# One weight tile in eight multiplied in full fp32, and the softmax row sums kept in SBUF instead of PSUM

## What is computed

```python
z = jnp.einsum('bhqd,bhkd->bhqk', qi, k).astype(jnp.float32) * scale
causal = key_pos[None, :] <= q_pos[:, None]
p = jax.nn.softmax(jnp.where(causal, z, neg), axis=-1)
return jnp.einsum('bhqk,bhkd->bhqd', p.astype(v.dtype), v)
```

## Time and profile before

| | |
|---|---|
| median of three runs | 2393.22 us (2389.26 to 2399.34) |
| profiled execution | 2389.26 us, of which 2387.6 us are the span of its instructions |
| mean granted TensorE clock, whole span | 0.913 |
| busy over the whole span | PE 1971.5 us, DVE 1342.3 us, ACT 952.6 us, POOL 595.2 us |
| MLA stage | 529 us, from 1646 to 2175 us |

### The profile page before, as it was taken

One profiled execution on the slowest core, in us unless ns is written; L12 is line 12 of the kernel. 1 busy time (PEld: TensorE's weight loads), 2 busy tenths in 40 slices (PEclk: granted clock), 3 DMA queues, 4 the chain that ended last, 5 costly groups with the idle time before them and its releaser, 6 DMA issues. The chain is left out here.

```text
span 2387.6 us, 32025 instructions
## 1 busy us (share of the span) xinstructions
PE 1971.5 (83%) x9698; PEld 1593.0 (67%) x9698; DVE 1342.3 (56%) x2006; ACT 952.6 (40%) x1876; POOL 595.2 (25%) x555
## 2 busy tenths in 40 slices
PE   6589999967777547755989888896999999995998
PEld 1368888856666446653766666674878788784786
DVE  2711111121111158876999999996888888884111
ACT  2411111121111123334666666664767676674000
POOL 1400000000000025540000000003767777673221
PEclk9699999978888779987999999996999999997999
DMA  7245543343323136666334251408315243404554
GB/s 276 85 132 175 165 127 127 110 166 106 110 103 107 74 112 197 201 199 151 71 87 103 53 130 32 110 22 181 72 38 120 56 106 79 115 8 152 176 176 158
DMA packets 220289, 284.59 MB, mean 119 GB/s; under 512 B 10736, under 2 KB 158496, under 8 KB 214544
## 3 DMA queue, kind: packets, MB, share of 16 engines
q1 hardware_dynamic: 217872, 274.96, 39.7%
q10 hardware_dynamic: 2304, 8.39, 0.9%
HBM read 164.56 MB, written 114.56 MB: 117 GB/s over the span
## 5 line engine op out<-in xcount | busy, mean ns | idle before, releaser
L1856 POOL TENSOR_TENSOR mla_wl<-mla_w,mla_wh 128x512 fp32r<-128x512 f32 (+1 forms) x320 | 373.8, 1182 | 152.7 <-ACT mla_wh L1892 145.1
L1488 DVE TENSOR_TENSOR_SCAN sb_w<-sb_kp,sb_w 128x512 f32<-128x512 f32 x192 | 245.2, 1277 | 7.2 <-ACT sb_kp L1438 0.9
L1447 ACT ACTIVATE sb_wh<-sb_pt 128x512 fp32r<-128x512 f32 (+1 forms) x320 | 170.5, 533 | 151.4 <-PE sb_pt L1580 147.5
L1891 ACT ACTIVATE mla_w<-mla_zt 128x512 f32<-128x512 f32 (+1 forms) x320 | 170.7, 533 | 119.9 <-PE mla_zt L2045 59.1
L515 PE MATMUL pt_po<-h_hi,pt_wh 128*128 128x512 f32 x512 | 200.5, 392 | 7.8 <-DVE pt_wl L476 7.8
L516 PE MATMUL pt_po<-h_lo,pt_wh 128*128 128x512 f32 x512 | 200.3, 391 | 0.0
L517 PE MATMUL pt_po<-h_hi,pt_wl 128*128 128x512 f32 x512 | 200.1, 391 | 0.0
L1933 DVE TENSOR_REDUCE mla_nmx<-mla_zn 128x1 f32<-128x512 f32 (+2 forms) x320 | 191.7, 601 | 11.2 <-PE mla_zn L2012 7.8
L1438 ACT ACTIVATE sb_kp<-sb_z 128x512 f32<-128x512 f32 (+3 forms) x320 | 169.7, 531 | 51.4 <-PE sb_z L1558 22.2
L716 PE MATMUL pn_pv<-pn_wh,pn_hs 128*128 128x512 f32 x256 | 104.5, 497 | 86.2 <-DMA pn_hs<-hT 86.2
L1580 PE MATMUL sb_pt<-sb_ident,sb_w 128*128 128x128 f32 x1088 | 174.6, 276 | 0.0
(11 more groups left out here) (221 smaller groups left out, 4381.9 us busy)
## 6 DMA issues: line engine op xcount, KB each, us to landing
pn_hs<-hT SPq DMA_DIRECT2D x16, 1024.0 KB, 11.2
mod_wada<-in_w_ada SPq DMA_DIRECT2D x6, 2048.0 KB, 8.4
qk_mla<-lat_th SPq DMA_DIRECT2D x32, 384.0 KB, 4.3
qk_mla<-lat_tl SPq DMA_DIRECT2D x32, 384.0 KB, 5.1
mod_x<-in_x ACTq DMA_DIRECT2D x16, 512.0 KB, 4.0
pt_w<-in_w_feat SPq DMA_DIRECT2D x16, 512.0 KB, 6.0
hT<-h_hi SPq DMA_DIRECT2D x16, 512.0 KB, 3.5
hT<-h_lo SPq DMA_DIRECT2D x16, 512.0 KB, 5.1
```

What stands on the lines that cost most here:

```text
L1447: nc.scalar.activation(wh[x % RING][:, lo:GW], pt[x % PTS][:, lo:GW], ACT.Copy, bias=-1.0).then_inc(s_hi if plan.split[x] else s_whole, 1)
L1488: nc.vector.tensor_tensor_scan(kept, keeps, keeps, 1.0 if u["n"] == 0 else w[u["g"]][:, u["r"], b:b + 1], ALU.mult, ALU.bypass).then_inc(s ...
L1856: nc.gpsimd.tensor_tensor(wl[i][:, cols], w[i][:, cols], wh[i][:, cols].bitcast(F32), ALU.subtract).then_inc(s_lo, 1)
L1891: nc.scalar.activation(w[i][:, cols], zt[x % 2][:, cols], ACT.Exp).then_inc(s_w, 1)
```

## The change

Two things are edited in `attend_mla` and its plan.

First, every eighth turn of a head (x = 7, 15, 23, 31, 39) is no longer split. ACT makes only w for it, POOL does nothing, and PE multiplies w with v as plain fp32, in one matmul instruction in place of two. Three of the five turns are of full width, two (15 and 39) have 128 columns.

Second, the running sum stays in the SBUF tile acc from the first turn on; the PSUM tile pa is gone. Its bank becomes a tile pm of its own for the transposed row maxima, so that some waits around the shared tile ps are dropped.

```diff
+    WHOLE = 8
...
+                split = len(self.turns) % self.WHOLE != self.WHOLE - 1
...
-        pa = m.ps("pa", [P, GW])
+        pm = m.ps("pm", [P, GW])
...
             def low(it, hp, x):
+                if not plan.turns[x]["split"]:
+                    return
...
-                pool.wait_ge(s_wh, turns(x, it, hp) + 1)
+                pool.wait_ge(s_wh, split_turns(x, it, hp))
...
-                nc.scalar.activation(wh[i][:, cols], zt[x % 2][:, cols], ACT.Exp).then_inc(s_wh, 1)
+                if plan.turns[x]["split"]:
+                    nc.scalar.activation(wh[i][:, cols], zt[x % 2][:, cols], ACT.Exp).then_inc(s_wh, 1)
...
-                nc.scalar.activation(qh[hp][QK:KP, g * GW:(g + 1) * GW], ps[0:1, :], ACT.Copy).then_inc(s_row, 1)
+                nc.scalar.activation(qh[hp][QK:KP, g * GW:(g + 1) * GW], pm[0:1, :], ACT.Copy).then_inc(s_row, 1)
...
-                if tn["first"]:
-                    nc.vector.tensor_copy((a if tn["diag"] else pa)[:], w[x % RING][:]).then_inc(s_acc, 1)
-                    return
-                dve.wait_ge(s_acc, turns(x, it, hp))
-                into = a if tn["diag"] else pa
-                came = a if tn["lowest"] else pa
-                nc.vector.tensor_tensor(into[:, cols], came[:, cols], w[x % RING][:, cols], ALU.add).then_inc(s_acc, 1)
+                    nc.vector.tensor_copy(a[:], w[x % RING][:]).then_inc(s_acc, 1)
+                else:
+                    dve.wait_ge(s_acc, turns(x, it, hp))
+                    nc.vector.tensor_tensor(a[:, cols], a[:, cols], w[x % RING][:, cols], ALU.add).then_inc(s_acc, 1)
...
-                reached(pe, s_scale, groups(n, it, hp) - (1 if n == 1 else 2))
...
-                pe.wait_ge(s_lo, turns(x, it, hp) + 1)
+                if not tn["split"]:
+                    pe.wait_ge(s_w, turns(x, it, hp) + 1)
+                    nc.tensor.matmul(out, vj.bitcast(F32), w[x % RING][:, lo:GW], start=tn["first"],
+                                     stop=tn["last"]).then_inc(s_pv, 1)
+                    return
+                pe.wait_ge(s_lo, split_turns(x, it, hp))
...
-                rows = groups(n, it, hp) + (2 if n == G - 1 else 3)
-                reached(pe, s_row, min(rows, 2 * PAIRS * G) if isinstance(rows, int) else rows)
```

More of the change, by code:

```diff
@@ L1640, in __init__ @@
             for j in range((g + 1) * QG):
-                self.turns.append(dict(n=n, g=g, j=j, lowest=max(0, j - g * QG), diag=(j >= g * QG),
+                split = len(self.turns) % self.WHOLE != self.WHOLE - 1
+                self.turns.append(dict(split=split, n=n, g=g, j=j, lowest=max(0, j - g * QG), diag=(j >= g * QG),
                                        first=(j == 0), last=(j == (g + 1) * QG - 1)))
@@ L1648, in __init__, with splits_to @@
         self.T, self.G = len(self.turns), len(self.groups)
+        self.splits = sum(tn["split"] for tn in self.turns)
+    def splits_to(self, x):
+        return sum(tn["split"] for tn in self.turns[:x + 1])
     def at(self, x, kinds, delays):
@@ L1753, in groups, with split_turns @@
             return it * (2 * G) + (hp * G + n)
+        def split_turns(x, it, hp):
+            return it * (2 * plan.splits) + (hp * plan.splits + (plan.splits_to(x) if x >= 0 else plan.splits_to(x + T) - plan.splits))
         def pair_groups(n, it):
@@ L1948, in add_up @@
                 dve.wait_ge(s_w, turns(x, it, hp) + 1)
-                if tn["diag"] and tn["lowest"] == 0:
+                if tn["first"]:
                     reached(dve, s_sum, groups(tn["n"], it, hp) - 1)
-                if tn["first"]:
-                    nc.vector.tensor_copy((a if tn["diag"] else pa)[:], w[x % RING][:]).then_inc(s_acc, 1)
-                    return
-                dve.wait_ge(s_acc, turns(x, it, hp))
-                into = a if tn["diag"] else pa
-                came = a if tn["lowest"] else pa
-                nc.vector.tensor_tensor(into[:, cols], came[:, cols], w[x % RING][:, cols], ALU.add).then_inc(s_acc, 1)
+                    nc.vector.tensor_copy(a[:], w[x % RING][:]).then_inc(s_acc, 1)
+                else:
+                    dve.wait_ge(s_acc, turns(x, it, hp))
+                    nc.vector.tensor_tensor(a[:, cols], a[:, cols], w[x % RING][:, cols], ALU.add).then_inc(s_acc, 1)
             def halves(it, hp, n):
@@ L2021, in to_row @@
                 reached(pe, s_row, groups(n, it, hp))
-                reached(pe, s_scale, groups(n, it, hp) - (1 if n == 1 else 2))
                 for r in range(QG):
-                    tp = nc.tensor.transpose(ps[0:1, r * P:(r + 1) * P], nm[n % 2][:, r:r + 1], ident[:])
+                    tp = nc.tensor.transpose(pm[0:1, r * P:(r + 1) * P], nm[n % 2][:, r:r + 1], ident[:])
                 tp.then_inc(s_pm, 1)
@@ L2036, in scores @@
                     pe.wait_ge(s_row, groups(tn["n"], it, hp) + 1)
-                reached(pe, s_wh, turns(x, it, hp) - 1)
+                if plan.turns[x - 2]["split"]:
+                    reached(pe, s_wh, split_turns(x - 2, it, hp))
+                else:
+                    reached(pe, s_w, turns(x, it, hp) - 1)
                 lo, g, keys = tn["lowest"] * P, tn["g"], slice(tn["j"] * P, (tn["j"] + 1) * P)
```

## The result

The changed kernel takes 2411.3 us (median of five runs, 2410.6 to 2416.3), the kernel before 2393.3 (five runs, 2389.3 to 2399.3). The ratio is 1.0074, with an interval of 1.0052 to 1.0094: **slower by 18 us**, where +37 was forecast. The sign and the range held; the size was twice too large. The profiled execution took 2413.95 us with a span of 2412.0, 24.4 us more than the span before. The whole of it lies in the MLA stage: its first tile is worked on at 1623.2 us before and 1623.0 after, its last is done at 2178.7 before and 2203.1 after.

The account below looks back on a forecast made before the run. PE was taken to set the pace, DVE just behind. Terms 11 + 0 + 0 + 4 + 20 + 5 = 40 us on 2389.26 gave 2429, forecast as 2430 us; range 2400 to 2482 us.

Parts of the forecast that it names:

- Where the loss comes from: Signs expected in the MLA profile: longer additions and POOL subtractions, DVE busier, ACT's quotient wait above 27 us, earlier stages unchanged.
- Whole products: PE in unsplit turns: fp32 product adds 0.39 us per full-width turn, 0.10 per narrow one; +11.0 us, bounds 0 and 20.
- Whole turns on ACT and POOL: ACT loses 14.2 us and POOL 31.6 us of work; PE waits for POOL only 2.3 us: 0, at best 10 off.
- Rival D: Group ends: the SBUF addition goes while POOL's subtraction waits, the quotient follows directly; faster, 2364 us, chance 0.06.
- The sum beside POOL: SBUF additions queue behind POOL at the port: +4 us in plain turns, +20 at odd heads' closing steps, +5 for clock.
- my terms without the clock: Port delays in the MLA stage: 0.5 us for a head, +4 us; 1.25 us for each of 16 group ends, +20.
- The narrow turns then let DVE catch up: Even heads: 0.8 us of delay left after the longest run is recovered in narrow turns, so most is absorbed.
- 1.2 us in hand: Full-width turns: how late DVE may be before PE wants the zn buffer again, about 1.2 us and no more.
- Clock: MLA stage: longer stalls lower the granted clock, a fifth more loss; +5 us, bounds -15 and +15.
- the prediction's own conversion: Stage clock 0.95 read as a tenth of 529 us at half speed, a loss of up to 26 us.

Follow-up runs that it names:

- e10: The kernel before, plus one semaphore increment that nobody reads on POOL ahead of each subtraction: 2369.7 us, ratio 0.9911.
- the narrow subtraction: The changed kernel with POOL's subtraction cut to the last 128 columns of each tile: 2370.9 us, ratio 0.9894.

## Why the prediction was right in sign and wrong in size

- **Where the loss comes from: right.** Additions of 1.076 us (0.95 to 1.1 expected), subtractions of 1.542, DVE +55 us (60), ACT's wait for the quotient 35.4 us (above 27), the stages before unchanged. Whoever is first at the port runs at full speed and the other stands, as the two rows 0.07 us apart, the quotients of `e10` and the narrow subtraction show. The Trainium skill states this lock on its page "SBUF — State Buffer", section "🔬 SBUF: two separate sides"; the traces agree.
- **Whole products, +11 us: right in kind, over in size.** The 0.39 us for each stands: without relief turn 10 of the first head, which holds the whole product of turn 7, takes 1.80 us in place of 1.40. In the whole kernel it is +6.7 us; where the other 4 went was not looked for.
- **"Whole turns on ACT and POOL ... so I take 0": this step failed.** It is the main error. I priced the relief by PE's waits for POOL, 2.3 us, and its best case at 10. The work that ACT and POOL no longer do is worth about 10 us in the change, and a thing that the diff does beside it, a register instruction more ahead of each subtraction, another 14, much of it by way of the clock. The second I never looked at: I listed the changed wait and priced only what it waits for, not when POOL would then start. Rival D had the mechanism, but put it down to the additions and gave it 0.06.
- **The sum beside POOL, 4 + 20 + 5 = 29 us: too small.** Alone it costs 38. As heads are cut in the table, three of the four closings fall into the odd head and one into the even head behind it, so my terms without the clock are 4.3 us for an odd head, 0.5 for the first head and 1.8 for the other even ones. Measured: odd heads +4.9, +9.4 and +6.3, the first head +2.4, the other even ones +6.4, +4.7 and +1.8. "The narrow turns then let DVE catch up" is where this failed. The 1.2 us in hand cover one delay in plain turns, but the diagonal's turns are shorter on PE and not by as much on DVE: in the first head of the kernel with the SBUF sum alone the turns 13 to 15 take 1.67, 1.64 and 1.86 us from one exponential to the next, against 1.17, 1.26 and 1.42 before. Behind odd heads DVE arrives late from their last group: at the start of head 2 the weight loads wait 2.3 us at once for a row maximum, where before 0.4 was the longest. How much of the even heads' time that is was not measured.
- **Clock, +5 us: right for the change, too small for the sum alone.** Over the stage it is 0.95 in both kernels, so next to nothing in the change. With the sum alone it is 0.92 in 576 us. That is about 92 us at half clock in place of 53, so by the prediction's own conversion up to 19 of the 38 us, an estimate. The whole turns brought this back, with the relief and the later start.
- **The forecast as a sum.** The terms for the sum and the wide product, 29 + 11 = 40 us, were too small in the one and too large in the other, and without relief both together measured 1.0174, 42 us. That these two errors nearly cancel is luck. Relief and race, forecast at 0, took 24 off: 42 - 24 = 18, as measured. So nearly all of the miss is the step taken as 0.

What stays open: how the 10 us of relief are shared between ACT and POOL. ACT's part was never tried alone, and with the sum in PSUM the relief of both was not tried without the later start; there the increment alone gives 21 us, more than the 17 that relief and later start gave together. The later start frees ten low parts without relief and four with it, for the same 14 us; why four are worth as much is not shown, beyond the clock. Nor is it shown why the low part wins the race in one kernel and the quotient in another; the start times of POOL move with all that stands before.

## What to carry to other kernels

A DVE operation with two inputs in SBUF beside a busy POOL is a race for a lock, not a share of bandwidth: look at which of the two starts first at each step on the path, and at everything that moves the start, the form of the waits included. Measure the two halves of a change apart before explaining its sum; here one half was +38 us and the other -10. And where an in-order engine stands waiting for a closing step, move that step one turn later first: this one edit of the old kernel was worth 1.5%, twice what the change lost.

## What the runs showed that I had not expected

- An idle semaphore increment on POOL ahead of each subtraction makes the whole kernel faster by 0.9%, because POOL then loses races that it had won by 0.07 us.
- The one that loses stands for what is left of the other: a DVE operation of 0.68 us takes 1.76, a subtraction of 1.28 takes 1.83. So it is cheaper to let DVE win: 0.55 us on an engine that has time, against 1.08 on one that has none.
- POOL's work is no measure of its busy time here: 40 of 320 subtractions fewer, and 10 us more busy, since the others stand at the port.
- A late closing step can cost more than its own lateness, by way of the clock: head 3 with two blocked low parts, 1.9 us late together, took 79.9 us at a clock of 0.90, and without them 71.2 at 0.98.
